# Expert-choice MoE layer on one core: gate and up in chunks of 512 inner columns, and the sample tokens' tiles of two chunks in one block

## The chip, the cores and the metric

The kernel runs on one core of a Trainium2 chip. Its time is the device time in microseconds of one execution; the median of three runs is compared. The profile is of one execution, taken by the hardware profiler.

## The reference

One layer of a bidirectional encoder runs on two request groups with the same weights: a prompt of 1024 tokens and a sample of 256 tokens, model width 1024, all fp32. First comes a mixer (projection to 2048, gated convolution, 2-D Fourier mixing, output projection, two norms). Then comes a mixture of 16 experts with inner width 2816, which takes most of the time. Each expert picks the tokens with the highest affinity to it, 128 of the prompt and 32 of the sample:

```
aff = jax.nn.softmax(logits, axis=-1)
cap = CAPACITY_FACTOR * t // N_EXPERTS          # 128 (prompt), 32 (sample)
gates, idx = lax.top_k(aff.T, cap)
xe = jnp.take(xt, idx, axis=0)
a = jnp.einsum("ecd,edf->ecf", xe, w_gate)      # (16, cap, 1024) x (16, 1024, 2816)
b = jnp.einsum("ecd,edf->ecf", xe, w_up)
ye = jnp.einsum("ecf,efd->ecd", jax.nn.silu(a) * b, w_down)
ye = ye * gates[..., None].astype(ye.dtype)
out = jnp.zeros_like(xt).at[idx.reshape(-1)].add(ye.reshape(-1, d))
```

The layer ends with a final norm of all tokens.

## The kernel before

The first 548 us hold the mixer, the router and the choice of tokens; the change does not touch them. Then the experts follow one after another: expert 0, a hardware loop over experts 1 to 14, and expert 15, all from the same function `expert`, written once per engine.

**Units.** The weights of an expert arrive in 33 units of 1 MB: 22 of the input stage (gate and up) and 11 of the down stage. `load_unit` on SyncE's queue fills a ring `raw` of 11 slots, 8 KB a partition each. An input unit holds 256 inner columns of up and of gate (a chunk, eleven to an expert) for half of the contraction, four of its eight 128-row pieces k; each row of it is a piece of 1 KB in memory. A down unit holds two inner blocks of 128 rows, with pieces of 4 KB. The first four units of expert 0 are loaded early.

**Two products from one load.** For the prompt tokens, each unit is split into a high half `spl_h` (ScalarE, L660) and a low half `spl_l` (VectorE, L1021), three units deep (`SPL`), and TensorE does three matmuls of 512 columns for each product in `three` (L315 to L317): high by high, high by low, low by high. The sample tokens are multiplied in plain fp32 straight from `raw`. They are only 32, so four matmuls share the array: each has 32 stationary columns and goes to its own 32 partitions of bank 2 (`sample_in`, L1289) or, in the down stage, of bank 6 (`sample_down`, L1301).

**Blocks.** TensorE does the sample work in blocks behind certain units. `ENDS` names the ten units that close one: 3, 7, 11, 15, 19 and 21 of the input stage, 24, 27, 30 and 32 of the down stage. In a block of the input stage it first turns the finished products of earlier chunks by transposes (`transposed`, L1263, and `transposed_s`, L1271), then samples the column tile of 512 columns (two chunks of 256) that just ended. Each block ends in one increment of `pe_s`, and only that frees the slots of its units:

```
sp.wait_ge(pe_s, e * BLOCKS + (block_of(i - RAW) + 1))
load_unit(e, i)
```

**Behind TensorE.** At the end of a chunk ScalarE takes silu of the gate half from PSUM (`silu_p`, L672) and only then splits the next unit; VectorE multiplies with the up half (L1031) ahead of its own split. The prompt's up and gate of a chunk share one bank (banks 0 and 1 in turn), the turned products go to banks 7 and 3, the down sums to banks 4 and 5. After unit 24 TensorE turns the gathered tokens of the next expert (`gathered`, L1250). At the expert's end ScalarE scales yP (L704) and yS (L725), and GpSimd adds both to the result in memory by indirect DMA (L494, L498), one after the other. After the last expert the result is read back, normed and written.

## Time and profile before

| | |
|---|---|
| median of three runs | 2610.35 us (2608.66 to 2610.88) |
| profiled execution | 2607.22 us, span 2605.4 us |
| TensorE busy | 2465.3 us (95%) |
| VectorE, ScalarE busy | 1661.5 us (64%), 1360.6 us (52%) |
| chain that ended last | TensorE 91%, VectorE 5%, the rest under 2% each |
| DMA queue of SyncE | 452176 packets, 598.88 MB, 68.0% of 16 engines |
| loads of gate and up | 352 each, 512 KB a load |
| loads of down | 176, 1024 KB a load |
| expert stage | from 548 to 2567 us |

Busy time of TensorE is modelled and its matmuls overlap in it (a mean of 390 ns for a matmul that follows its neighbour by 227 ns), so its cost is read from starts, not from means. A wait is put down to what came last.

### The profile page before, as it was taken

The page shows a single profiled execution, that of the slowest core. Times are in us where ns is not written, and L with a number is a line of the kernel's source. Part 1 is how long each engine was busy: PE and PEld are TensorE (multiplying, and loading weights), DVE is VectorE, ACT ScalarE, POOL GpSimd, SP SyncE. Part 2 cuts the span into 40 slices and gives each one's busy share as a digit, 9 for nine tenths or more (in the row PEclk, how much of TensorE's full clock was granted, in tenths as well). Part 3 has the DMA queues.
Part 4 walks back from the last instruction along what each step waited for, and adds up shares of the span by engine and source line. Part 5 has one row for each costly group of instructions (what it writes and reads, how often), then busy time and mean ns, then how long its engine had stood idle before and what let it go on. Part 6 is the DMA issues. An engine that isn't in the chain of part 4 may idle for free.

```text
span 2605.4 us, 46448 instructions
## 1 busy us (share of the span) xinstructions
PE 2465.3 (95%) x18269; PEld 1903.4 (73%) x18269; DVE 1661.5 (64%) x1541; ACT 1360.6 (52%) x1473; POOL 269.2 (10%) x191
## 2 busy tenths in 40 slices
PE   5999779669999999999999999999999999999994
PEld 4888768547777777777777777777777777777772
DVE  4344456966666666666676666676766676666663
ACT  5222323336555555555565656565555565565553
POOL 0010120010202020202020201111020202020000
PEclk8999989779999999999999999999999999999997
DMA  3110253537979798989798888888888888888885
GB/s 117 41 40 17 106 167 114 178 110 281 294 281 291 277 285 292 284 292 284 279 287 289 280 295 285 286 290 284 270 295 281 292 288 287 292 284 292 256 289 180
DMA packets 460734, 627.31 MB, mean 241 GB/s; under 512 B 21392, under 2 KB 400528, under 8 KB 460304
## 3 DMA queue, kind: packets, MB, share of 16 engines
q1 hardware_dynamic: 452176, 598.88, 68.0%
q0 software_dynamic: 8384, 25.71, 3.9%
q8 instruction: 157, 2.57, 0.4%
q14 instruction: 17, 0.14, 0.0%
HBM read 598.31 MB, written 26.21 MB: 240 GB/s over the span
## 4 chain that ended last, share of the span: by engine, by line
PE 91%; DVE 5%; DMA 1%; ACT 1%; issue 1%; POOL 0%; SPq 0%; POOLq 0%; DVEq 0%; ACTq 0%
PE ps L315 21%; PE ps L316 20%; PE ps L317 20%; PE ps L1289 12%; PE ps L1105 9%; PE ps L1301 6%; PE ps L1263 1%; DVE i L896 1%; DVE v L894 1%; DVE A L898 1%; DMA wo_raw<-in_w_out_dram 1%; PE ps L1250 1%; DVE fo L1083 0%; PE ps L1271 0%; DVE wof_l L834 0%
## 5 line engine op out<-in xcount | busy, mean ns | idle before, releaser
L1021 DVE TENSOR_TENSOR spl_l<-raw,spl_h 128x2048 fp32r<-128x2048 f32 x528 | 1210.1, 2292 | 653.2 <-ACT spl_h L660 633.9
L660 ACT ACTIVATE spl_h<-raw 128x2048 fp32r<-128x2048 f32 x528 | 1010.8, 1915 | 559.5 <-PE ps L317 559.4
L315 PE MATMUL ps<-spl_h,xT 128*128 128x512 f32 x1408 | 559.3, 397 | 2.5 <-DVE xT L1026 2.5
L317 PE MATMUL ps<-spl_h,xT 128*128 128x512 f32 x1408 | 549.8, 390 | 0.0
L316 PE MATMUL ps<-spl_l,xT 128*128 128x512 f32 x1408 | 549.4, 390 | 0.0
L315 PEld LDWEIGHTS ps<-spl_h,xT 128*128 128x128 f32 x1408 | 264.6, 188 | 94.3 <-issue 41.6
L1289 PE MATMUL ps<-raw,xTs 128*32 128x256 f32 (+1 forms) x6144 | 324.1, 363 | 0.0
L317 PEld LDWEIGHTS ps<-spl_h,xT 128*128 128x128 f32 x1408 | 264.7, 188 | 56.0
L316 PEld LDWEIGHTS ps<-spl_l,xT 128*128 128x128 f32 x1408 | 264.8, 188 | 52.4
L315 PE MATMUL ps<-spl_h,g 128*128 128x512 f32 x704 | 281.8, 400 | 0.0
L316 PE MATMUL ps<-spl_l,g 128*128 128x512 f32 x704 | 275.3, 391 | 0.0
L317 PE MATMUL ps<-spl_h,g 128*128 128x512 f32 x704 | 274.2, 390 | 0.0
L1289 PEld LDWEIGHTS ps<-raw,xTs 128*32 128x32 f32 x6144 | 185.2, 110 | 112.3 <-issue 16.1
L494 POOL DMA_INDIRECT acc_dram<-yP,sidx x16 | 26.0, 1624 | 1780.5 <-ACT yP L704 1780.5
L315 PEld LDWEIGHTS ps<-spl_h,g 128*128 128x128 f32 x704 | 132.0, 188 | 49.3 <-issue 22.9
L1301 PE MATMUL ps<-raw,gs 128*32 128x256 f32 x2816 | 165.2, 381 | 0.0
L317 PEld LDWEIGHTS ps<-spl_h,g 128*128 128x128 f32 x704 | 132.2, 188 | 28.6
L316 PEld LDWEIGHTS ps<-spl_l,g 128*128 128x128 f32 x704 | 132.2, 188 | 25.5
L672 ACT ACTIVATE sv<-ps 128x256 f32<-128x256 f32 x176 | 67.7, 385 | 151.5 <-PE ps L317 151.5
L1301 PEld LDWEIGHTS ps<-raw,gs 128*32 128x32 f32 x2816 | 85.0, 110 | 69.1 <-issue 19.6
L1105 PE MATMUL ps<-hT_h,win_h 128*128 128x512 f32 (+1 forms) x384 | 96.4, 359 | 5.9 <-DVE win_l L771 5.9
L1105 PE MATMUL ps<-hT_l,win_h 128*128 128x512 f32 (+1 forms) x384 | 96.2, 359 | 0.0
(195 smaller groups left out, 2170.5 us busy)
## 6 DMA issues: line engine op xcount, KB each, us to landing
raw<-in_w_up_dram SPq DMA_DIRECT2D x352, 512.0 KB, 6.1
raw<-in_w_gate_dram SPq DMA_DIRECT2D x352, 512.0 KB, 7.3
raw<-in_w_down_dram SPq DMA_DIRECT2D x176, 1024.0 KB, 8.8
win_raw<-in_w_in_dram SPq DMA_DIRECT2D x16, 512.0 KB, 3.8
xt<-in_x_dram SPq DMA_DIRECT2D x10, 512.0 KB, 8.2
xr<-in_x_dram SPq DMA_DIRECT2D x10, 512.0 KB, 4.0
acc_dram<-xr SPq DMA_DIRECT2D x10, 512.0 KB, 2.6
xn_dram<-xn SPq DMA_DIRECT2D x10, 512.0 KB, 2.9
```

Source lines behind the costliest of these rows:

```text
L315: eng.matmul(o, a_h, b_h, start=first, stop=False, skip_group_check=True)
L316: eng.matmul(o, a_h, b_l, start=False, stop=False, skip_group_check=True)
L317: return eng.matmul(o, a_l, b_h, start=False, stop=last, skip_group_check=True)
L660: act.activation(spl_h[:, i % SPL, :], raw[:, slot_of(i), :], ACT.Copy).then_inc(sh_ok, 1)
L672: act.activation(sv[:, :], bank(c % 2)[:, FW:2 * FW], ACT.Silu).then_inc(s_ok, 1)
L894: dve.max(v[0:n, rs], A[0:n, :]).then_inc(top_ok[h], 1)
L896: dve.max_index(idx[0:n, rs], v[0:n, rs], A[0:n, :]).then_inc(top_ok[h], 1)
L898: dve.match_replace(A[0:n, :], v[0:n, rs], A[0:n, :], -2.0).then_inc(top_ok[h], 1)
L1021: dve.tensor_tensor(spl_l[:, i % SPL, :], raw[:, slot_of(i), :], spl_h[:, i % SPL, :].bitcast(F32), ALU.subtract).then_inc(sl_ok, 1)
L1105: last = pe.matmul(u[:, t0:t1], w[:, slot, k, :], h[:, k, t0:t1], start=(k == 0 and i == 0), stop=(k == KD - 1 and i == 2), skip_group_che ...
L1289: last = pe.matmul(o, xTs[:, k, :], w, start=k == 0, stop=k == KD - 1, skip_group_check=True)
L1301: last = pe.matmul(bank(6)[q * CAPS:(q + 1) * CAPS, 0:DQ], gs[:, f, :], raw[:, slot_of(i), b * D + q * DQ:b * D + (q + 1) * DQ], start=f = ...
```

## The change

Gate and up come in six chunks: chunk 0 has 256 inner columns in two units as before, chunks 1 to 5 have 512 in four units each, every unit with two k of them. The rows of a wide chunk are pieces of 2 KB. The prompt's up and gate of a wide chunk have a bank each (banks 4 and 5 for odd chunks, 0 and 1 for even ones), and three matmuls of 512 columns go to the one, three to the other for each k. Chunk 0 has bank 3. The down sums move to banks 0 and 1, the gathered tokens' transposes to banks 4 and 5.

The sample work is done in five blocks, behind units 5, 13, 21, 28 and 32. A block of the input stage samples two chunks, into the two halves of bank 2. `pe_s` still rises once for each chunk sampled, and once for each down block, so that a chunk's slots come free when its own sampling is done. silu, product and turned halves are done once a chunk, 512 columns wide. `TURNS` names the block in which each chunk is turned. `sv`, `svs` and `pvs` get new places.

The core of the diff:

```diff
@@ -29,15 +29,21 @@
 E = 16
 F = 2816
 FB = F // P
-NC = FB // 2
+HID = 4 * P
+NC = F // HID + 1
+INS = 4 * NC - 2
 CAP, CAPS = 2 * SEQ // E, 2 * DEC // E
 C = CAP + CAPS
-UNITS = 3 * NC
+UNITS = INS + FB // 2
 FW = 2 * P
 KH = KD // 2
-BATCHES = (NC + 1) // 2
-ENDS = [min(4 * b + 3, 2 * NC - 1) for b in range(BATCHES)] + [2 * NC + 2, 2 * NC + 5, 2 * NC + 8, UNITS - 1]
-BLOCKS = len(ENDS)
+LASTS = [1 + 4 * c for c in range(NC)]
+BATCH = ((0, 1), (2, 3), (4, 5))
+NB = len(BATCH)
+DOWNS = (INS + 6, UNITS - 1)
+ENDS = [LASTS[b[-1]] for b in BATCH] + list(DOWNS)
+TURNS = [min(n for n in range(len(ENDS)) if ENDS[n] > LASTS[c]) for c in range(NC)]
+SAMPLE = NC + len(DOWNS)
 UNIT = 2 * D
 QS = P // CAPS
 DQ = D // QS
...
@@ -165,10 +171,10 @@
         xgs = at("xgs", 90 * KB, [P, DQ])
         yP = at("yP", 94 * KB, [P, D])
         yS = at("yS", 98 * KB, [P, DQ])
-        pv = at("pv", 110 * KB, [P, 3, FW])
-        sv = at("sv", 113 * KB, [P, FW])
-        svs = at("svs", 114 * KB, [P, P])
-        pvs = at("pvs", 114 * KB + 512, [P, P])
+        pv = at("pv", 110 * KB, [P, 3, HID])
+        sv = at("sv", 108 * KB, [P, HID])
+        svs = at("svs", 205 * KB, [P, 2, P])
+        pvs = at("pvs", 75 * KB, [P, 2, P])
 
         fx = at("fx", 117 * KB, [P, TILES, D])
...
+        def first_block(c):
+            return 4 * c - 2 if c else 0
+
+        def blocks(c):
+            return 4 if c else 2
+
+        def first_unit(c):
+            return LASTS[c - 1] + 1 if c else 0
+
+        def chunk_of(i):
+            return (i + 2) // 4
+
+        def up_bank(c):
+            if c == 0:
+                return bank(3)[:, 0:FW]
+            return bank((0, 4)[c % 2])
+
+        def gate_bank(c):
+            if c == 0:
+                return bank(3)[:, FW:2 * FW]
+            return bank((1, 5)[c % 2])
+
+        def turned(c):
+            return bank((3, 7)[c % 2])[:, 0:blocks(c) * P].rearrange("p (b n) -> p b n", b=blocks(c))
+
+        def turned_s(b):
+            return bank(3 if b == NB - 1 else 6)
+
+        def batch_blocks(b):
+            first = first_block(BATCH[b][0])
+            return first, sum(blocks(c) for c in BATCH[b])
+
         def three(eng, o, a_h, a_l, b_h, b_l, first, last):
 
             eng.matmul(o, a_h, b_h, start=first, stop=False, skip_group_check=True)
...
@@ -353,14 +391,17 @@
 
 
             def load_unit(e, i):
-                if i < 2 * NC:
-                    fs = slice((i // 2) * FW, (i // 2 + 1) * FW)
-                    ks = slice((i % 2) * KH, (i % 2 + 1) * KH)
-                    dst = raw[:, slot_of(i), :].rearrange("p (k f) -> p k f", k=KH)
-                    sp.dma_start(dst[:, :, 0:FW], up_v[e, :, ks, fs]).then_inc(raw_in[slot_of(i)], 16)
-                    sp.dma_start(dst[:, :, FW:2 * FW], gate_v[e, :, ks, fs]).then_inc(raw_in[slot_of(i)], 16)
+                if i < INS:
+                    c = chunk_of(i)
+                    w, kn = blocks(c) * P, KD // blocks(c)
+                    fs = slice(first_block(c) * P, first_block(c) * P + w)
+                    r = i - first_unit(c)
+                    ks = slice(r * kn, (r + 1) * kn)
+                    dst = raw[:, slot_of(i), :].rearrange("p (k f) -> p k f", k=kn)
+                    sp.dma_start(dst[:, :, 0:w], up_v[e, :, ks, fs]).then_inc(raw_in[slot_of(i)], 16)
+                    sp.dma_start(dst[:, :, w:2 * w], gate_v[e, :, ks, fs]).then_inc(raw_in[slot_of(i)], 16)
                 else:
-                    j = i - 2 * NC
+                    j = i - INS
...
+            def released(i):
+                if i < INS:
+                    return chunk_of(i) + 1
+                return NC + min(n for n in range(len(DOWNS)) if DOWNS[n] >= i) + 1
 
             for i in range(EARLY, UNITS):
                 if i >= RAW:
-                    sp.wait_ge(pe_s, block_of(i - RAW) + 1)
+                    sp.wait_ge(pe_s, released(i - RAW))
                 load_unit(0, i)
             with nc.Fori(1, E, engines=(sp.engine,), hint_back_edge=True) as e:
                 for i in range(UNITS):
                     if i < RAW:
-                        sp.wait_ge(pe_s, e * BLOCKS + (block_of(i - RAW + UNITS) + 1 - BLOCKS))
+                        sp.wait_ge(pe_s, e * SAMPLE + (released(i - RAW + UNITS) - SAMPLE))
                     else:
-                        sp.wait_ge(pe_s, e * BLOCKS + (block_of(i - RAW) + 1))
+                        sp.wait_ge(pe_s, e * SAMPLE + released(i - RAW))
                     load_unit(e, i)
...
             def silu_p(e, c):
-                act.wait_ge(pe_unit, e * UNITS + (2 * c + 2))
-                if not (isinstance(e, int) and e == 0 and c == 0):
-                    act.wait_ge(p_ok, e * NC + c)
-                act.activation(sv[:, :], bank(c % 2)[:, FW:2 * FW], ACT.Silu).then_inc(s_ok, 1)
+                act.wait_ge(pe_unit, e * UNITS + (LASTS[c] + 1))
+                act.activation(sv[:, 0:blocks(c) * P], gate_bank(c), ACT.Silu).then_inc(s_ok, 1)
 
             def silu_s(e, b):
-                act.wait_ge(pe_s, e * BLOCKS + (b + 1))
-                if not (isinstance(e, int) and e == 0 and b == 0):
-                    act.wait_ge(pS_ok, e * BATCHES + b)
-                if b < BATCHES - 1:
-                    act.activation(svs[:, :], bank(2)[:, P:2 * P], ACT.Silu).then_inc(sS_ok, 1)
+                act.wait_ge(pe_s, e * SAMPLE + (BATCH[b][-1] + 1))
+                n = len(BATCH[b])
+                if b == 0:
+                    act.activation(svs[0:64, 0, :], bank(2)[64:P, 0:P], ACT.Silu).then_inc(sS_ok, 1)
+                    act.activation(svs[:, 1, :], bank(2)[:, FW + P:2 * FW], ACT.Silu).then_inc(sS_ok, 1)
                 else:
-                    act.activation(svs[0:64, :], bank(2)[64:P, 0:P], ACT.Silu).then_inc(sS_ok, 1)
+                    act.activation(svs[:, 0:n, :], bank(2)[:, 0:n * FW].rearrange("p (n m f) -> p n m f", n=n, m=2)[:, :, 1, :],
+                                   ACT.Silu).then_inc(sS_ok, 1)
 
             def product_hi(e, c):
                 act.wait_ge(pT_ok, e * NC + (c + 1))
-                gb = g[:, 2 * c * GB:(2 * c + 2) * GB].rearrange("p (b n) -> p b n", b=2)
-                act.activation(gb[:, :, P:2 * P], bank((7, 3)[c % 2])[:, 0:FW].rearrange("p (b n) -> p b n", b=2),
-                               ACT.Copy).then_inc(gh_ok, 1)
+                f, w = first_block(c), blocks(c)
+                gb = g[:, f * GB:(f + w) * GB].rearrange("p (b n) -> p b n", b=w)
+                act.activation(gb[:, :, P:2 * P], turned(c), ACT.Copy).then_inc(gh_ok, 1)
 
             def product_s(e, b):
-                act.wait_ge(sT_ok, e * BATCHES + (b + 1))
-                if b < BATCHES - 1:
-                    act.wait_ge(pT_ok, e * NC + (2 * b + 2))
-                w = 4 if b < BATCHES - 1 else 2
-                act.activation(gs[:, 4 * b:4 * b + w, :], bank(3)[:, FW:FW + w * CAPS].rearrange("p (b n) -> p b n", b=w),
+                f, w = batch_blocks(b)
+                act.wait_ge(sT_ok, e * NB + (b + 1))
+                act.activation(gs[:, f:f + w, :], turned_s(b)[:, 0:w * CAPS].rearrange("p (b n) -> p b n", b=w),
                                ACT.Copy).then_inc(gs_ok, 1)
...
+                    if i in LASTS:
+                        silu_p(e, LASTS.index(i))
...
+                    if i in ENDS:
                         b = ENDS.index(i)
-                        if b > 0:
+                        for c in range(NC):
+                            if TURNS[c] == b:
+                                product_hi(e, c)
+                        if 0 < b <= NB:
                             product_s(e, b - 1)
-                            product_hi(e, 2 * b - 1)
-                        if b < BATCHES - 1:
-                            product_hi(e, 2 * b)
-                        silu_s(e, b)
-                    if i == ENDS[BATCHES]:
-                        product_s(e, BATCHES - 1)
-                        product_hi(e, NC - 1)
-                        if not last:
+                        if b < NB:
+                            silu_s(e, b)
...
+            dve.memset(pvs[:, 0, :], 0.0).then_inc(pS_ok, 1)
...
+            def prompt_in(e, i):
+                c = chunk_of(i)
+                w, kn = blocks(c) * P, KD // blocks(c)
+                for kk in range(kn):
+                    k = (i - first_unit(c)) * kn + kk
+                    u = slice(kk * 2 * w, (kk + 1) * 2 * w)
+                    wh, wl = spl_h[:, i % SPL, u], spl_l[:, i % SPL, u]
+                    if c == 0:
+                        last = three(pe, bank(3), xT[:, 0, k, :], xT[:, 1, k, :], wh, wl, k == 0, k == KD - 1)
+                    else:
+                        for m, o in enumerate((up_bank(c), gate_bank(c))):
+                            ms = slice(m * w, (m + 1) * w)
+                            last = three(pe, o, xT[:, 0, k, :], xT[:, 1, k, :], wh[:, ms], wl[:, ms], k == 0, k == KD - 1)
+                last.then_inc(pe_unit, 1)
...
+            def sample_in(e, c, n):
+                w, kn = blocks(c) * P, KD // blocks(c)
                 for k in range(KD):
+                    i = first_unit(c) + k // kn
+                    u = raw[:, slot_of(i), (k % kn) * 2 * w:(k % kn + 1) * 2 * w]
                     for q in range(QS):
-                        if b < BATCHES - 1:
-                            unit = 4 * b + 2 * (q // 2) + k // KH
-                            w = raw[:, slot_of(unit), (k % KH) * 2 * FW:(k % KH + 1) * 2 * FW]
-                            w = w.rearrange("p (m h f) -> p h m f", m=2, h=2)[:, q % 2, :, :]
-                            o = bank(2)[q * CAPS:(q + 1) * CAPS, 0:2 * P]
+                        o = bank(2)[q * CAPS:(q + 1) * CAPS, n * FW:(n + 1) * FW]
+                        if c == 0:
+                            o, v_ = o[:, 0:P], u[:, q * P:(q + 1) * P]
                         else:
-                            unit = 4 * b + k // KH
-                            w = raw[:, slot_of(unit), (k % KH) * 2 * FW + q * P:(k % KH) * 2 * FW + (q + 1) * P]
-                            o = bank(2)[q * CAPS:(q + 1) * CAPS, 0:P]
-                        last = pe.matmul(o, xTs[:, k, :], w, start=k == 0, stop=k == KD - 1, skip_group_check=True)
+                            v_ = u.rearrange("p (m f) -> p m f", m=2)[:, :, q * P:(q + 1) * P]
+                        last = pe.matmul(o, xTs[:, k, :], v_, start=k == 0, stop=k == KD - 1, skip_group_check=True)
                 last.then_inc(pe_s, 1)
 
-            def sample_down(e, n):
-                if n == 0:
-                    pe.wait_ge(yS_ok, e + 1)
-                first, end = (2 * NC if n == 0 else ENDS[BATCHES + n - 1] + 1), ENDS[BATCHES + n]
-                pe.wait_ge(gs_ok, e * BATCHES + ((end - 2 * NC) // 2 + 1))
...
+            def turn(e, c):
+                pe.wait_ge(p_ok, e * NC + (c + 1))
+                if c or not (isinstance(e, int) and e == 0):
+                    pe.wait_ge(gl_ok, e * NC + max(c - 1, 0))
+                for b in range(blocks(c)):
+                    last = pe.transpose(turned(c)[:, b, :], pv[:, c % 3, b * P:(b + 1) * P], ident[:, :])
+                last.then_inc(pT_ok, 1)
+
...
+                    if i == 0:
+                        pe.wait_ge(xTl_ok, e + 1)
+                        if later:
+                            pe.wait_ge(gs_ok, e * NB)
+                    if i == first_unit(2) and later:
+                        pe.wait_ge(yP_ok, e)
+                    if i < INS:
+                        prompt_in(e, i)
                     else:
-                        j = i - 2 * NC
-                        pe.wait_ge(gl_ok, e * NC + (j + 1))
-                        if j == 0 and not (isinstance(e, int) and e == 0):
-                            pe.wait_ge(yP_ok, e)
-                        for b in range(2):
-                            f = 2 * j + b
-                            p_lo, p_hi = g[:, f * GB:f * GB + P], g[:, f * GB + P:(f + 1) * GB]
-                            for n in range(2):
-                                ds = slice(b * D + n * 512, b * D + (n + 1) * 512)
-                                last = three(pe, bank(4 + n), p_hi, p_lo, spl_h[:, slot, ds], spl_l[:, slot, ds],
-                                             f == 0, f == FB - 1)
-                    last.then_inc(pe_unit, 1)
-                    if i in ENDS[0:BATCHES]:
-                        b = ENDS.index(i)
-                        if b > 0:
-                            transposed_s(e, b - 1)
-                            transposed(e, 2 * b - 1)
-                        if b < BATCHES - 1:
-                            transposed(e, 2 * b)
-                        sample_in(e, b)
-                    if i in ENDS[BATCHES:]:
-                        if i == ENDS[BATCHES]:
-                            transposed_s(e, BATCHES - 1)
-                            transposed(e, NC - 1)
-                            if not last_expert:
-                                gathered(e + 2)
-                        sample_down(e, ENDS.index(i) - BATCHES)
+                        f = 2 * (i - INS) + 1
+                        pe.wait_ge(gl_ok, e * NC + (min(c for c in range(NC) if first_block(c) + blocks(c) > f) + 1))
+                        prompt_down(e, i)
+                    if i not in ENDS:
+                        continue
+                    b = ENDS.index(i)
+                    for c in range(NC):
+                        if TURNS[c] == b:
+                            turn(e, c)
+                    if b == 1 and later:
+                        pe.wait_ge(yS_ok, e + 1)
+                    if 0 < b <= NB:
+                        turn_s(e, b - 1)
+                    if b == NB and not last_expert:
+                        gathered(e + 2)
+                    if b == 0:
+                        pe.wait_ge(xTs_ok, e + 1)
+                    if b < NB:
+                        for n, c in enumerate(BATCH[b]):
+                            sample_in(e, c, n)
+                    else:
+                        first = INS if b == NB else ENDS[b - 1] + 1
+                        f = 2 * (i - INS) + 1
+                        pe.wait_ge(gs_ok, e * NB + (min(n for n in range(NB) if sum(batch_blocks(n)) > f) + 1))
+                        sample_down(e, first, i)
```

## Rows read from the trace of the kernel before

**Rows 1.** The stretch of one expert; columns in the first line; busy times in us.

```profile
core 0: us, PE busy (x) PEld busy (x) DVE busy (x) ACT busy (x) POOL busy (x), PEclk, DMA share, GB/s
1264.50:1390.68 126.18, 126.18 (x995) 94.99 (x995) 85.25 (x62) 74.55 (x73) 14.21 (x10) 1.00 0.86 285
```

**Rows 2.** The waits of the expert stage, 548 to 2567 us.

```profile
DVE spl_l L1021 <- ACT spl_h L660: 633.9, 443, 4.7
...
PE ps L315 <- DVE xT L1026: 2.5, 1, 2.5
PEld ps L315 <- DVE spl_l L1021: 0.4, 1, 0.4
```

**Rows 3.** Part 5 of the page, three of the costliest groups: busy us, mean ns of one | idle before.

```profile
L1021 DVE TENSOR_TENSOR spl_l<-raw,spl_h 128x2048 fp32r<-128x2048 f32 x528 | 1210.1, 2292 | 653.2 <-ACT spl_h L660 633.9
...
L1289 PE MATMUL ps<-raw,xTs 128*32 128x256 f32 (+1 forms) x6144 | 324.1, 363 | 0.0
...
L1301 PE MATMUL ps<-raw,gs 128*32 128x256 f32 x2816 | 165.2, 381 | 0.0
```

**Rows 4.** The chain of waits of two experts: start us, us, what.

```profile
1207.28 3.59 PE ps L1289 x64
...
1262.61 1.88 PE ps L1289 x64
1264.50 0.43 PE ps L315
1273.21 0.87 PE ps L1250 x8
1274.30 2.73 PE ps L1301 x48
...
1305.01 1.86 PE ps L1301 x32
...
1390.68 0.43 PE ps L315
```

**Rows 5.** The timeline of TensorE around a sample block: start us, us.

```profile
1206.34 0.39 PE L317 MATMUL ps<-spl_h,xT 128*128 128x512 f32 x1
...
1207.21 3.66 PE L1289 MATMUL ps<-raw,xTs 128*32 128x256 f32 x64
...
1211.61 0.39 PE L315 MATMUL ps<-spl_h,xT 128*128 128x512 f32 x1
...
1221.59 0.39 PE L317 MATMUL ps<-spl_h,xT 128*128 128x512 f32 x1
```

**Rows 6.** The same around a block of the down stage.

```profile
1285.03 0.39 PE L317 MATMUL ps<-spl_h,g 128*128 128x512 f32 x1
...
1288.89 0.40 PE L315 MATMUL ps<-spl_h,g 128*128 128x512 f32 x1
```

**Rows 7.** The timeline of SyncE's DMA queue.

```profile
1211.07 0.37 SPq L360 DMA_DIRECT2D raw<-in_w_up_dram  x1
1211.54 0.46 SPq L361 DMA_DIRECT2D raw<-in_w_gate_dram  x1
```

**Rows 8.** The DMA issues of L361, 1211 to 1226 us, issue to landing.

```profile
DMA to landing us min/median/max: 5.0/6.9/8.7
```

**Rows 9.** Two stretches of transfers alone; columns as in rows 1.

```profile
1218.00:1219.00 1.00, 1.00 (x6) 0.84 (x5) 0.55 (x3) 0.85 (x1) 0.00 (x0) 1.00 1.10 346
1248.00:1250.00 2.00, 2.00 (x10) 1.68 (x9) 1.55 (x3) 1.55 (x2) 0.00 (x0) 1.00 1.02 416
```

**Rows 10.** The timeline of ScalarE at the end of a chunk.

```profile
1216.65 0.39 ACT L672 ACTIVATE sv<-ps 128x256 f32<-128x256 f32 x1 [0.88 <-PE ps L317]
1216.93 1.91 ACT L660 ACTIVATE spl_h<-raw 128x2048 fp32r<-128x2048 f32 x1
```

**Rows 11.** The chain of waits at the end.

```profile
2565.84 1.12 ACT yP L704
...
2569.63 6.19 DMA acc_dram<-yS,sidx
```

More of the change, by code:

```diff
@@ L703, in expert @@
                         act.wait_ge(cg_ok, e * 4 + 4)
-                        act.activation(yP[:, :], bank(4, 2), ACT.Copy, scale=cgate[:, 0:1]).then_inc(yP_ok, 1)
+                        act.activation(yP[:, :], bank(0, 2), ACT.Copy, scale=cgate[:, 0:1]).then_inc(yP_ok, 1)
                     n = i + SPL
@@ L1044, in expert @@
+                gb = g[:, f * GB:(f + w) * GB].rearrange("p (b n) -> p b n", b=w)
+                dve.tensor_tensor(gb[:, :, 0:P], turned(c), gb.bitcast(F32)[:, :, P:2 * P], ALU.subtract).then_inc(gl_ok, 1)
             def expert(e, last):
                 for i in range(UNITS):
-                    if i < 2 * NC and i % 2:
-                        product(e, i // 2)
+                    if i in LASTS:
+                        product(e, LASTS.index(i))
                     n = i + SPL
@@ L1253, in gathered @@
                 last.then_inc(xg_ps, 1)
-            def transposed(e, c):
-                pe.wait_ge(p_ok, e * NC + (c + 1))
-                if c >= 2:
-                    pe.wait_ge(gl_ok, e * NC + (c - 1))
-                elif c == 0 and not (isinstance(e, int) and e == 0):
-                    pe.wait_ge(gl_ok, e * NC)
-                for b in range(2):
-                    bs = slice(b * P, (b + 1) * P)
-                    last = pe.transpose(bank((7, 3)[c % 2])[:, bs], pv[:, c % 3, bs], ident[:, :])
-                last.then_inc(pT_ok, 1)
@@ new lines, in prompt_down @@
+            def prompt_down(e, i):
+                for b in range(2):
+                    f = 2 * (i - INS) + b
+                    p_lo, p_hi = g[:, f * GB:f * GB + P], g[:, f * GB + P:(f + 1) * GB]
+                    for n in range(2):
+                        ds = slice(b * D + n * 512, b * D + (n + 1) * 512)
+                        last = three(pe, bank(n), p_hi, p_lo, spl_h[:, i % SPL, ds], spl_l[:, i % SPL, ds],
+                                     f == 0, f == FB - 1)
+                last.then_inc(pe_unit, 1)
@@ L1304, in sample_down, with turn_s @@
                 last.then_inc(pe_s, 1)
+            def turn(e, c):
[5 more added lines that the diff above has]
+                last.then_inc(pT_ok, 1)
+            def turn_s(e, b):
+                pe.wait_ge(pS_ok, e * (NB + 1) + (b + 3))
+                if b or not (isinstance(e, int) and e == 0):
+                    pe.wait_ge(gs_ok, e * NB + b)
+                o = 0
+                for n, c in enumerate(BATCH[b]):
+                    last = pe.transpose(turned_s(b)[:, o:o + P], pvs[:, n, :], ident[:, :])
+                    o += blocks(c) * CAPS
+                last.then_inc(sT_ok, 1)
@@ L1306, in expert @@
             def expert(e, last_expert):
+                later = not (isinstance(e, int) and e == 0)
                 for i in range(UNITS):
                     pe.wait_ge(sl_ok, e * UNITS + (i + 1))
[L1309 to L1332 removed]
```

81 lines of the change are left out of this document (30 added, 51 removed).

## The prediction

> **What bounds the kernel now.** I read the split by engine over one expert first. From one expert's first down matmul to the next's is 126.18 us, TensorE is busy for all of it at granted clock 1.00 (its upper level, 2.4 GHz), VectorE for 85.25 us, ScalarE for 74.55 us, and the DMA engines' mean share is 0.86 [rows 1]. Sixteen such stretches are 2019 of the 2605.4 us. Then the waits: between 548 and 2567 us TensorE waits once for data, 2.5 us at the very start, and its weight loads 0.4 us, while VectorE waits 633.9 us for ScalarE [rows 2]. The reader is to see that nothing feeds TensorE late, so the time is the sum of what TensorE issues. Last, the chain of waits and TensorE's timeline, to find in that sum what is not arithmetic.
>
> The prices, start to start. A 128x512 matmul: 44 of them from 1211.61 to 1221.59, 0.2268 us [rows 5]. A transpose: 8 in 0.87, 0.109 us. A 256-wide sample instruction: 48 take 2.73 and 32 take 1.86, so 0.0544 each and 0.12 us fixed; 64 take 3.59, which gives 0.11 fixed. The 128-wide ones: (1.88 - 0.11) / 64 = 0.0277 [rows 4]. (Each fp32 sample matmul of the source is two instructions.)
>
> Now a whole switch to sample work and back. From the last prompt matmul (1206.34) to the fourth after the block (1211.61) is 5.27 us; it holds four matmuls (0.907), five transposes (0.545) and 64 sample instructions (3.482), together 4.93, so **0.34 us belong to the switch** [rows 5, 4]. In the down stage, with no transposes, 1285.03 to 1288.89 is 3.86 us against 0.907 + 48 x 0.0544 = 3.52: again 0.34 [rows 6]. As a check, an expert has 396 prompt matmuls (22 units and 11 units of 12), 38 transposes, 5 x 64 and 176 wide and 64 narrow sample instructions: 89.8 + 4.1 + 17.4 + 9.6 + 1.8 = 122.7 us. What is left of 126.18 is 3.5 us, over ten blocks 0.35 each.
>
> **The change, part by part.**
>
> *Blocks, ten to five.* ENDS had six blocks in the input stage and four in the down stage; it now has units 5, 13, 21, 28 and 32. The matmuls, transposes and sample instructions of an expert stay the same in number and width (a chunk of 512 has two matmuls of 512 in place of one per k, over half as many k per unit). Five switches an expert go: 5 x 16 x 0.34 = 27.2 us. With 0.35, from the check, it is 28.0.
>
> The row shows that the 0.34 us come alike with transposes and without, and whether 48 or 64 instructions follow; so I take them as a price of the change of kind, paid once a block however long. The Trainium skill (TensorEngine Tiling (Array Packing), Key Properties) says that "Changing tiling mode (not just tile) drains the TensorE". By that the two chunks sampled one after the other, both in 32-column tiles, cost nothing between them, and the sum stays 27.2 us; if instead each chunk's sampling paid its fixed part, it would be the second rival below.
>
> *The last expert's tail.* The chain ends through yP, GpSimd's queue and the DMA of yS, which starts 3.8 us after yP [rows 11]. The sample work behind the last prompt matmul is hidden there: 32 instructions before, 64 after. So 32 x 0.0544 = 1.74 us more lie behind yP, and only about 0.3 us of it show (the block then ends 0.2 + 3.5 us behind the last prompt matmul, yS takes some 0.4 like the equally wide sv [rows 10], together 4.2 with the signal, against 0.2 + 3.8 = 4.0 us at which the queue comes free). Gain 1.4 us.
>
> *Wider silu, product and halves.* Eleven pairs of evictions become six, wider; VectorE and ScalarE lose about 2 us of work per expert each, and gain nothing for the end, since they have 41 and 52 us free [rows 1]. Without that cover it would still be a gain. What counts is their lead at a chunk's end that no block follows (units 9 and 17). The silu starts 0.27 us into the next unit (1216.65 against 1211.61 + 21 x 0.2268 = 1216.37), the split 0.28 us behind it [rows 10]. At 512 columns the silu is longer by about 256 x (1.12 - 0.39) / 768 = 0.24 us, with the 1024-wide yP as the far row [rows 10, 11]. So the split starts at 0.79, takes 1.91, VectorE's half 2.29 [rows 3], and it is ready at 5.0 us; TensorE wants it after two units, at 5.44. Covered, by 0.4 us. Priced at nothing; with the cover gone, what it is late by, 32 times.
>
> *Two accumulators in turn.* In a wide chunk TensorE alternates between two banks every three matmuls. The down stage does so now, and its matmuls run at the same 0.2268 us at clock 1.00. The Trainium skill (TensorE: Matmul & The Clock Gate, A second HAM failure mode) says that cycling through banks can make the clock swing between its levels; here the trace disagrees, and only a small chance stays for it.
>
> *Pieces of 2 KB and the ring of 11 slots.* This is the edit that could cost. SyncE waits for a slot until its sampling is done, and a block now holds 6 to 8 units in place of 4. Take block 1 (units 6 to 13), T being the end of its prompt work. Units 14 to 16 are there; unit 17 waits for chunk 2's sampling. That ends at 0.1 (today's gap ahead of the first sample instruction, 1207.21 - 1206.34 - 0.227 - 0.545) + 10 x 0.109 + 0.12 + 3.48 = T + 4.8 [rows 5, 4]. Today the first gate piece goes out at 1211.54 and lands 5.0 us later, 1216.5, which is 5.7 us after the sampling ended at 1210.87 [rows 4, 7, 8]: unit 17 lands at T + 10.5. The others follow at the rate of the transfers: 346 GB/s with 1 KB pieces, or 3.0 us for the 1.05 MB of a unit, and 416 GB/s with the 4 KB pieces of the down weights, 2.5 us [rows 9]. 2 KB has no row; it lies between, and I take the middle, 2.75 us. TensorE ends chunk 3's sampling at T + 8.3 and unit 14 at 11.1; ScalarE can take unit 17 at 11.4, and each next one 2.72 us later, with 0.9 us to spare (1.92 + 2.29 against two units, 5.44, and the 0.27 of the signal). The last of the batch, 21, may land as late as 11.4 + 10.9 + 0.9 = T + 23.2. It lands at 10.5 + 4 x 2.75 = 21.5; at today's rate 22.5. Covered either way; the ring starts to hurt above 3.17 us a unit. The same walk after unit 21 brings 4 KB pieces, which are faster; after unit 28 seven slots free at once ahead of 22 us of work. The waits that are added (gs_ok, gl_ok, yP_ok, yS_ok) are for work finished a block earlier.
>
> *Sum.* 27.2 + 1.4 = **28.6 us** off the profiled execution's 2607.22 us (span 2605.4, 1.8 us around it): 2578.6. That execution lies 3.1 us under the median shown, so on the median's scale 2610.35 - 28.6 = 2581.7; I say 2581.5.
>
> **Rivals.**
> 1. *The ring starves TensorE (the other side).* For: 11 slots, 8 held, only 3 ahead, and the DMA's mean share is 0.86 already. Against: the walk above. Place: units 17 to 21. Its price is 16 x 4 x (r - 3.17) us with r the time of a unit. It eats all the gain at r = 3.62 us, 290 GB/s. At r = 3.8, slower than any steady stretch of rows 9, it is 40 us: 2621.7. A mild form, r = 3.3, gives 8 us: 2590.
> 2. *The fixed 0.12 us stay with each chunk's sampling.* Then the three merges of the input stage bring 0.22 each: 48 x 0.12 = 5.8 us less gain, 2587.5. Against: rows 5 and 6 price a switch alike.
> 3. *The lead at chunk ends is gone.* For: 0.4 us is little, and VectorE's wider product stands ahead of its split. 0.3 us late, 32 times: 9.6 us, 2591.
> 4. *The clock falls with the banks in turn.* If wholly, the 240 wide-chunk matmuls of an expert would take twice 0.2268 us: +871 us, about 3450.
> 5. *The change moves nothing*: some wait I have not found takes 1.5 to 2 us an expert back, 2605 to 2615.
>
> **How the numbers follow.** Forecast 0.70 (its own range 2579 to 2585: a switch from 0.32 to 0.36 us, and 1.5 us of scatter), rival 2 0.07, rival 3 0.06, rival 1 mild 0.05 and strong 0.06, rival 4 0.01, rival 5 0.05. The range is to hold the first four, 0.88 of the chance, up to 13 us above the forecast: 2576 to 2595. The lower end is a switch of 0.35 and a profile-like execution. 0.2% (5.2 us) is about what a measurement of this kernel tells from no change. Faster: 0.70 + 0.07 + 0.06 + 0.05 = 0.88; same: rival 5, 0.05; slower: strong rival 1 and rival 4, 0.07.
>
> **What would show it.** Right: an expert takes 124.5 us; five blocks in the chain of waits, with 128 sample instructions at 0.0544 (or 0.0277) us behind each other and no gap where the second chunk begins; a first L315-like matmul of 0.43 us five times an expert, not ten. TensorE still waits for nothing. Wrong: waits of TensorE for VectorE's lower half at units 17 to 21 (rival 1, with SyncE's issues bunched after each block) or at units 12 and 20 (rival 3); a second 0.1 us inside the blocks (rival 2). The transfers between two blocks should run above 346 GB/s; if they run below 330 the walk of the ring fails.

## The result and the profile after

The changed kernel takes **2579.67 us** (median of 4 runs, 2579.22 to 2580.67) against 2609.81 us for the kernel before (4 runs, 2608.66 to 2610.88): 30.1 us less, ratio 0.9885, 95% interval 0.9868 to 0.9902. The forecast was 2581.5 us, range 2576 to 2595. The profiled execution took 2579.22 us with a span of 2577.3 us, 28.1 us under the span before.

One expert in the split by engine, the row that answers to [rows 1]:

```profile
core 0: us, PE busy (x) PEld busy (x) DVE busy (x) ACT busy (x) POOL busy (x), PEclk, DMA share, GB/s
1158.92:1283.44 124.52, 124.52 (x996) 95.61 (x995) 84.49 (x50) 73.57 (x56) 8.11 (x10) 1.00 0.80 290
```

TensorE is still busy for the whole of it at granted clock 1.00, VectorE and ScalarE have 0.8 and 1.0 us less to do, and the DMA engines' share fell from 0.86 to 0.80 though they move the same bytes. The chain of waits over that expert (start us, us, what), beside [rows 4]:

```profile
1152.74 6.18 PE ps L1344 x112
1158.92 0.43 PE ps L353
...
1170.05 3.59 PE ps L1344 x64
...
1190.54 5.34 PE ps L1336 x128
...
1219.00 7.04 PE ps L1336 x128
1226.04 0.43 PE ps L353
...
1249.16 7.04 PE ps L1336 x128
...
1277.26 6.18 PE ps L1344 x112
1283.44 0.43 PE ps L353
```

Five blocks in place of ten. The sample instructions keep their price: 64 more in a wide block cost 7.04 - 3.59 = 3.45 us, 0.0539 each, and 112 take 6.18 where 112 x 0.0544 is 6.09. Over many experts, by the transposes of the gathered tokens, which come once an expert (14 of them from the first to the last row, from the same view over 700 to 2500 us):

```profile
778.39 0.87 PE ps L1295 x8
...
2396.02 0.87 PE ps L1295 x8
```

(2396.02 - 778.39) / 13 = 124.43 us an expert against 126.18 [rows 1]: 1.75 us less, 0.35 for each of the five switches that went. Sixteen times that is 28.0 us. The intervals are not all alike. Five of these thirteen are 124.44 to 124.64 us, the others 124.38 or 124.39, for instance

```profile
1649.33 0.87 PE ps L1295 x8
...
1773.72 0.87 PE ps L1295 x8
```

and the one before the first row is 125.37. Together the fourteen are 1.7 us longer than fourteen of the shortest. So an expert that is not held up takes 124.38 us, 1.80 less than before, and the runs below show what that is made of.

A switch by itself in TensorE's timeline, beside [rows 5]:

```profile
1217.51 0.39 PE L355 MATMUL ps<-spl_h,xT 128*128 128x512 f32 x1
1217.74 1.03 PE L1354 MATMUL ps<-ident,pv 128*128 128x128 f32 x8
1218.61 0.38 PE L1363 MATMUL ps<-ident,pvs 128*128 128x128 f32 x2
1218.92 7.11 PE L1336 MATMUL ps<-raw,xTs 128*32 128x256 f32 x128
...
1226.79 0.40 PE L353 MATMUL ps<-spl_h,xT 128*128 128x512 f32 x1
```

From 1217.51 to 1226.79 is 9.28 us; four matmuls (0.91), ten transposes (1.09) and 128 sample instructions (6.96) are 8.96. The switch costs 0.32 us by this count (0.34 in the rows before), although the block is twice as long and samples two chunks.

What changed for the worse is in the waits from 545 to 2545 us:

```profile
ACT spl_h L704 <- DMA raw<-in_w_gate_dram: 122.0, 122, 3.1
...
PE ps L353 <- DVE xT L1065: 2.5, 1, 2.5
...
PE ps L353 <- DVE spl_l L1060: 0.7, 1, 0.7
```

ScalarE now waits for the transfers 122 times, which it did not do before. TensorE feels it once by itself, for 0.7 us, and its weight loads wait four times, 2.0 us in all (0.4 before, [rows 2]); the uneven intervals above say that 1.7 us of the experts' time were lost. How near it is shows in ScalarE's timeline (the splits of units 17, 18 and 21, then of unit 5 of the next expert; the brackets hold the idle time before and its releaser):

```profile
1229.06 1.92 ACT L704 ACTIVATE spl_h<-raw 128x2048 fp32r<-128x2048 f32 x1 [2.57 <-PE ps L355]
1232.19 1.92 ACT L704 ACTIVATE spl_h<-raw 128x2048 fp32r<-128x2048 f32 x1 [1.21 <-DMA raw<-in_w_gate_dram]
...
1240.32 1.92 ACT L704 ACTIVATE spl_h<-raw 128x2048 fp32r<-128x2048 f32 x1 [0.69 <-DMA raw<-in_w_gate_dram]
...
1307.35 1.92 ACT L704 ACTIVATE spl_h<-raw 128x2048 fp32r<-128x2048 f32 x1 [1.30 <-DMA raw<-in_w_gate_dram]
```

With T = 1217.74, the end of the block's prompt work, unit 17 is taken at T + 11.3, unit 18 at 14.5 and unit 21 at 22.6, the last two as soon as they land. The forecast's walk had 11.4 for the first, and let unit 18 land at 10.5 + 2.75 = 13.3 and unit 21 at 21.5, with 23.2 as the limit: both came 1.1 to 1.2 us later than it said, and 0.6 us of cover is left in place of 1.7. Unit 5 is ready at 1307.35 + 1.92 + 0.03 + 2.29 = 1311.6, and TensorE starts it at 1311.82: 0.2 us of cover, at a place that the walk had called ample.

The transfers, a stretch of 2 KB pieces alone (columns as above), beside [rows 9]:

```profile
1206.00:1208.00 2.00, 2.00 (x11) 1.65 (x10) 1.71 (x1) 1.20 (x3) 0.00 (x0) 1.00 1.05 384
```

384 GB/s, between the 346 of 1 KB pieces and the 416 of 4 KB, and a unit takes 2.73 us. The page counts 296891 packets in place of 460734.

The end, beside [rows 11], from the timeline:

```profile
2537.77 1.11 ACT L745 ACTIVATE yP<-ps,cgate 128x1024 f32<-128x1024 f32 x1 [6.18 <-PE ps L355]
...
2541.39 0.47 ACT L764 ACTIVATE yS<-ps,cgate 128x256 f32<-128x256 f32 x1 [2.51 <-PE ps L1344]
2542.66 1.55 POOL L542 DMA_INDIRECT acc_dram<-yS,sidx  x1 [1.40 <-ACT yS L764]
```

The add of yS starts 4.9 us behind yP, not 3.8. Before, yS was ready when GpSimd came free from the add of yP; now GpSimd waits 1.4 us for yS.

### The profile page after: what moved, and what is told of

It reads as the page before. It is cut to its first block, busy times and chain, and to the rows that moved or that the text cites. A ratio compares the mean times of both kernels' runs of the same rounds, so it can differ in the third digit from the quotient of the medians.

```text
span 2577.3 us, 45156 instructions
## 1 busy us (share of the span) xinstructions
PE 2438.6 (95%) x18269; PEld 1915.0 (74%) x18269; DVE 1650.2 (64%) x1350; ACT 1344.1 (52%) x1233; POOL 194.7 (8%) x191
## 2 busy tenths in 40 slices
DMA packets 296891, 627.28 MB, mean 243 GB/s; under 512 B 21392, under 2 KB 72848, under 8 KB 296464
## 4 chain that ended last, share of the span: by engine, by line
PE 90%; DVE 5%; DMA 2%; ACT 1%; issue 1%; SPq 0%; POOL 0%; DVEq 0%; ACTq 0%; POOLq 0%
PE ps L353 20%; PE ps L354 19%; PE ps L355 19%; PE ps L1336 12%; PE ps L1150 9%; PE ps L1344 6%; PE ps L1354 1%; DVE i L935 1%; DVE v L933 1%; DVE A L937 1%; DMA raw<-in_w_gate_dram 1%; PE ps L1295 1%; DMA wo_raw<-in_w_out_dram 1%; DVE wof_l L873 0%; PE ps L1363 0%
## 5 line engine op out<-in xcount | busy, mean ns | idle before, releaser
L1336 PE MATMUL ps<-raw,xTs 128*32 128x256 f32 (+1 forms) x6144 | 314.2, 362 | 0.0
L1344 PE MATMUL ps<-raw,gs 128*32 128x256 f32 x2816 | 158.6, 380 | 0.0
L1150 PE MATMUL ps<-hT_h,win_l 128*128 128x512 f32 (+1 forms) x384 | 96.2, 359 | 0.0
```

Of the source, the lines that this page charges most:

```text
L1150: last = pe.matmul(u[:, t0:t1], w[:, slot, k, :], h[:, k, t0:t1], start=(k == 0 and i == 0), stop=(k == KD - 1 and i == 2), skip_group_che ...
L1336: last = pe.matmul(o, xTs[:, k, :], v_, start=k == 0, stop=k == KD - 1, skip_group_check=True)
L1344: last = pe.matmul(bank(6)[q * CAPS:(q + 1) * CAPS, 0:DQ], gs[:, f, :], raw[:, slot_of(i), b * D + q * DQ:b * D + (q + 1) * DQ], start=f = ...
```

## The experiments

Two theories stood against each other: the gain is the price of the switches between prompt and sample work, or it is the wide chunks (2 KB pieces, six wide evictions in place of eleven pairs). Each run below is timed against the kernel before on the same chip; its own median stands with the ratio's interval. The runs were made in batches on different chips; the kernel before had medians of 2609.4 to 2609.9 us in them, so a difference from the changed kernel's 2579.67 carries about 0.5 us from there, and a median also holds what changes outside the expert stage.

**Four down blocks in the changed kernel.**

```diff
-DOWNS = (INS + 6, UNITS - 1)
+DOWNS = (INS + 2, INS + 5, INS + 8, UNITS - 1)
```

> The changed kernel, but the down stage has four sample blocks again (behind units 24, 27, 30 and 32) in place of two; all else stays, the wide chunks too. Theory (a switch of TensorE between prompt and sample work costs 0.34 us, and the change gains by having fewer of them): 2 x 16 x 0.34 = 10.9 us, and 1.4 us because less sample work hides behind yP at the end: 2579.7 + 12.3 = 2592. Rival (the gain comes from the wide chunks: 2 KB pieces, fewer and wider evictions): within 2 us of 2579.7.

Measured: 2593.32 us, ratio 0.9937 (0.9924 to 0.9951), 13.7 us over the changed kernel. This is the theory of the switches; the rival of the wide chunks (within 2 us of 2579.7) fails. Its experts are all of one length, by the same rows:

```profile
1271.06 0.87 PE ps L1295 x8
...
1396.24 0.87 PE ps L1295 x8
```

125.18 us, 0.80 above the 124.38 of the changed kernel: 0.40 for each of the two down blocks.

**Two down blocks in the kernel before.**

```diff
-ENDS = [...] + [2 * NC + 2, 2 * NC + 5, 2 * NC + 8, UNITS - 1]
+ENDS = [...] + [2 * NC + 6, UNITS - 1]
```

> The kernel before, with one thing of the change alone: the down stage has two sample blocks (behind units 28 and 32) in place of four; chunks stay at 256 columns and 1 KB pieces. Theory of the switch: 2609.8 - 10.9 - 1.4 = 2597.5. Rival of the wide chunks: 2609.8, no change.

Measured: 2595.65 us, ratio 0.9946 (0.9933 to 0.9960), 14.2 us under the kernel before. One line of the old kernel, changed, brings nearly half of the gain, with 256-wide chunks and 1 KB pieces. Its experts all take 125.39 or 125.40 us, 0.79 less than 126.18: again 0.40 a down block.

**Six input blocks in the changed kernel.** Behind a chunk's last unit that closes no block:

```diff
+if i in LASTS and i not in ENDS:
+    b = LASTS.index(i) // 2
+    if b == 0:
+        pe.wait_ge(xTs_ok, e + 1)
+    else:
+        pe.wait_ge(pS_ok, e * (NB + 1) + (b + 2))
+    sample_in(e, BATCH[b][0], 0)
...
-for n, c in enumerate(BATCH[b]):
-    sample_in(e, c, n)
+sample_in(e, BATCH[b][1], 1)
```

> The changed kernel, but each chunk is sampled right behind its own last unit: six sample blocks in the input stage in place of three; the transposes stay where they are. Theory of the switch: 3 x 16 x 0.34 = 16.3 us more, 2596. If the fixed 0.12 us of a block belong to each chunk's sampling (my second rival), they are paid already and only 0.22 us a block come back: 10.6 us, 2590. Rival of the wide chunks: 2579.7. The transfers should also start earlier, so ScalarE should wait less for them.

Measured: 2598.38 us, ratio 0.9956 (0.9942 to 0.9969), 18.7 us over the changed kernel, 0.39 for each of 48 blocks. My second rival (0.22 a block, 2590) is out. Its shortest intervals are 125.46 us, 1.08 above the changed kernel's: 0.36 for each of three input blocks. ScalarE's waits for gate transfers fell from 122.0 us to 52.2 us in the profile's waits.

**Ten blocks, wide chunks.** Both edits together.

> The changed kernel with both of the above: ten sample blocks an expert as before the change, but wide chunks. It closes the account. Theory of the switch: 2579.7 + 16.3 + 12.3 = 2608.3, so the wide chunks by themselves are worth 1.5 us or less against 2609.8. Rival of the wide chunks: near 2580, nearly all the gain stays.

Measured: 2611.90 us, ratio 1.0007 (0.9998 to 1.0016). That is 3.6 us over the theory's 2608.3 and about 2 us over the kernel before: with ten blocks the wide chunks gain nothing. The two edits add up (13.7 + 18.7 = 32.4 us, and both together cost 32.2). All its experts take 126.26 us:

```profile
1276.16 0.87 PE ps L1295 x8
...
1402.42 0.87 PE ps L1295 x8
```

So the wide chunks cost 0.08 us an expert, the two down switches are worth 126.26 - 125.46 = 0.80 and the three input switches 126.26 - 125.18 = 1.08, and 0.80 + 1.08 - 0.08 = 1.80 us is what the change takes off an expert that is not held up.

**What a switch is made of: the transposes between the two samplings.**

```diff
+if b < NB:
+    sample_in(e, BATCH[b][0], 0)
 for c in range(NC):
     if TURNS[c] == b:
         turn(e, c)
...
 if b < NB:
-    for n, c in enumerate(BATCH[b]):
-        sample_in(e, c, n)
+    sample_in(e, BATCH[b][1], 1)
```

(with a wait for xTs_ok or pS_ok ahead of the first sampling)

> The changed kernel, but in the three input blocks the transposes (full array, fp32) stand between the sampling of the block's first and second chunk, in place of ahead of both. The same instructions, and the slots of the first chunk come free up to 1.1 us earlier. It asks what the 0.34 us belong to. Theory (to the change between full-width work and 32-column tiles): one more change there and back in each input block, 48 x 0.34 = 16.3 us, 2596. Rival (to the change between the split prompt data and plain fp32, which the transposes share with the sample work): no change, 2580.

Measured: 2593.11 us, ratio 0.9939 (0.9925 to 0.9952), 13.4 us over the changed kernel or 0.28 for each of the 48 spells (by its shortest intervals, 125.10 and 125.11, it is 0.24). TensorE's timeline of this kernel:

```profile
1221.55 3.66 PE L1336 MATMUL ps<-raw,xTs 128*32 128x256 f32 x64
1225.14 1.09 PE L1354 MATMUL ps<-ident,pv 128*128 128x128 f32 x8
1226.07 0.38 PE L1363 MATMUL ps<-ident,pvs 128*128 128x128 f32 x2
1226.38 3.66 PE L1336 MATMUL ps<-raw,xTs 128*32 128x256 f32 x64
```

Each 64 now take 3.59 us (0.11 over 64 x 0.0544), and the ten transposes 1.24 instead of 1.09. So most of the price is paid when full-width work and 32-column tiles change places, also where both are plain fp32. The kind of the data doesn't explain it alone. Whether the 0.1 us between these 0.24 to 0.28 and the 0.36 of an input switch belongs to the split data was not tried, nor what in the change costs: a tile's place in the array, or the narrower weight loads.

**How near the ring is: 1 KB pieces.** Each load of a wide chunk in two DMAs, by columns; and as a control in two DMAs by k.

```diff
+for h in range(2 if c else 1):
+    n = 2 * P
+    o = first_block(c) * P + h * n
+    sp.dma_start(dst[:, :, m * w + h * n:m * w + (h + 1) * n],
+                 src[e, :, ks, o:o + n]).then_inc(raw_in[slot_of(i)], 16)
```

> The changed kernel, but every load of a wide chunk is cut by columns into two DMAs of 1 KB pieces (four DMAs a unit; same bytes, same places, same blocks). It asks how much cover the ring has. In the trace of the changed kernel ScalarE takes unit 18 at 14.5 us and unit 21 at 22.6 us behind the block's last prompt matmul, both times released by the DMA, where my walk had 13.3 and 21.5; the limit was 23.2. At the 346 GB/s of 1 KB pieces (3.0 us a unit in place of 2.7) unit 21 comes 1.5 us later, at 24.1: TensorE waits 0.9 us an expert, 14 us, 2594. My walk on record, 22.5 at this rate, says covered: 2580.

> The control of the 1 KB run: also four DMAs a unit, but cut by k, so that the pieces stay at 2 KB. If the size of the pieces is what counts: within 2 us of 2579.7. If it is the number of DMAs that SyncE issues, it is as slow as the 1 KB run.

Measured: with 1 KB pieces 2616.85 us, ratio 1.0024 (1.0014 to 1.0035); the control 2582.91 us, ratio 0.9895 (0.9880 to 0.9910). The control is 3.2 us over the changed kernel, more than the 2 I allowed, but its trace does not put this on the four DMAs a unit: from the first prompt matmul of the experts to the last yP it takes 1988.79 us (549.89 to 2538.68), the changed kernel 1989.01 (548.76 to 2537.77). The difference lies in the mixer and behind the experts. Against the control the pieces' size costs 34 us, more than the whole gain, and far more than either of my numbers. The chain of waits of the 1 KB kernel shows where:

```profile
1163.86 6.22 PE ps L1349 x112
...
1202.71 5.34 PE ps L1341 x128
...
1231.17 3.63 PE ps L1341 x64
...
1262.25 7.04 PE ps L1341 x128
1290.35 6.23 PE ps L1349 x112
...
1332.25 5.34 PE ps L1341 x128
```

From the block of unit 28 to that of the next expert's unit 5 it takes 38.85 and 41.90 us; the changed kernel has 1190.54 - 1152.74 = 37.80. From the block of unit 13 to that of 21 it takes 31.08 against 30.16. The second is what I had worked out, 0.9 us. The first I had not looked at: the freed slots are filled there without a pause, while GpSimd's gather and adds use the same engines. In this kernel's split by engine:

```profile
1189.00:1192.00 3.00, 3.00 (x15) 2.49 (x14) 2.31 (x2) 2.20 (x3) 2.13 (x1) 1.00 1.03 238
1216.00:1219.00 3.00, 3.00 (x15) 2.49 (x14) 2.58 (x2) 1.92 (x1) 0.00 (x0) 1.00 1.10 348
...
1327.00:1332.00 5.00, 4.59 (x14) 3.48 (x14) 3.39 (x3) 3.18 (x3) 0.00 (x0) 0.66 1.10 348
```

With GpSimd's DMA at work (2.13 us busy in the first) the engines are as full but move 238 GB/s, not 348. The changed kernel shows the same with 2 KB pieces: 261 GB/s from 1303 to 1306 us, with GpSimd busy for 2.69 us, against 384. How much of the loss is the sharing and how much the slower pieces was not separated.

The third row holds something else. TensorE had just waited 2.35 us, until 1327.41; behind that the mean granted clock is 0.66, a stretch at the lower level, 1.2 GHz, in which seven matmuls follow each other by 0.43 us in place of 0.23, 1.4 us lost. So this wait cost more than its own length, and the two are most of the 4.1 us that this expert lost there (41.90 - 37.80). The trace has one more such stretch, in the second expert; the changed kernel has none between 560 us and the end of the experts.

**The down slots free earlier.** Blocks behind 27 and 32 in place of 28 and 32, once in the changed kernel and once with 1 KB pieces.

```diff
-DOWNS = (INS + 6, UNITS - 1)
+DOWNS = (INS + 5, UNITS - 1)
```

> The changed kernel, but the down blocks stand behind units 27 and 32 in place of 28 and 32: still five blocks, six and five down units in them, so that the first down slots come free 3.5 us earlier (one unit of 2.72 us and 16 sample instructions less). TensorE's work is the same. In the changed kernel ScalarE takes unit 5 of the next expert when the DMA lets it, and its two halves are ready at about 1311.6 us, where TensorE wants it at 1311.8: hardly covered, yet covered. Theory: 2579.7, at most 1 us less. Rival (small waits there still cost the changed kernel something that its trace hides): 2575 to 2578.

> The 1 KB run (2616.9 us) with the down blocks behind 27 and 32. In the 1 KB run's chain of waits an expert loses about 1.3 us between its predecessor's block of unit 28 and its own first block, where the transfers run without a pause and the gather and the adds of GpSimd go over the same engines, and about 0.75 us between the blocks of units 13 and 21. Theory (both places are ring starvation, and the first goes when its slots come free 3.5 us earlier): 16 x 1.3 = 21 us less, 2596. Rival (1 KB pieces are too slow by their mean rate, so that the loss only moves to the next block): within 5 us of 2616.9.

Measured: 2579.93 us, ratio 0.9887 (0.9872 to 0.9902), for the first: the same as the changed kernel by the median. Its trace says a little more: its experts all take 124.40 or 124.41 us, so the 1.7 us that the changed kernel's profiled execution lost in places are not lost here. The medians are too coarse to tell whether the thin cover costs that. 2590.41 us, ratio 0.9931 (0.9917 to 0.9944), for the second: 26.4 us less than with the block behind 28. So most of the 34 us was starvation at the expert's start. What is left, 10.5 us over the same blocks with 2 KB pieces or 0.66 an expert, is of the size of the other place. The kernel before with two down blocks has 1 KB pieces too, and its even experts show no loss; there a sample block behind unit 3 stands ahead of unit 5, so that unit 5 is wanted later.

**Slots given back by the block.**

```diff
-return chunk_of(i) + 1
+return chunk_of(i) // 2 * 2 + 2
```

> The changed kernel, but the slots of a block's units are given back only when both of its chunks are sampled, in place of chunk by chunk; TensorE's work is the same. The transfers of units 17 and on then start 3.5 us later. Theory (the ring has well under 2 us to spare behind a wide block, and the finer release is what keeps TensorE fed): unit 21 comes at 26.1 against a limit of 23.2, so TensorE waits 2.9 us there, and about as long behind the block of unit 21: 16 x 5.8 = 93 us, 2672; if the 4 KB pieces of the down stage make up for the second, 2626. Rival (the ring has cover to spare, the release doesn't matter): 2580.

Measured: 2654.52 us, ratio 1.0171 (1.0157 to 1.0185): 74.9 us over the changed kernel, 4.7 an expert. The chain of waits:

```profile
1241.15 7.09 PE ps L1336 x128
...
1272.92 7.09 PE ps L1336 x128
...
1302.51 6.18 PE ps L1344 x112
```

Here 31.77 us from unit 13's block to unit 21's (30.16 in the changed kernel) and 29.59 from there to unit 28's (28.10). TensorE waits at both places, as forecast, but about half as long each here. Other experts lose more: in the next one the second stretch takes 33.39 us,

```profile
1400.60 7.09 PE ps L1336 x128
...
1433.99 6.18 PE ps L1344 x112
```

with a granted clock of 0.66 from 1420 to 1425 us, behind the wait. The release chunk by chunk is a necessary part of the change.

**Silu three times as long.**

```diff
-act.activation(sv[:, 0:blocks(c) * P], gate_bank(c), ACT.Silu).then_inc(s_ok, 1)
+w = blocks(c) * P
+act.activation(sv[:, :, 0:w], gate_bank(c).unsqueeze(1).broadcast_to([P, 3, w]), ACT.Silu).then_inc(s_ok, 1)
```

> The changed kernel, but silu goes over its columns three times in one instruction (1536 in place of 512; the product uses the last third), so ScalarE is about 1.0 us longer at each chunk's end. The changed kernel's trace has the split of unit 20 ready 0.44 us before TensorE wants it. Theory (that lead is 0.4 us at units 12 and 20 and ample elsewhere): 1.0 - 0.44 = 0.55 us late, 32 times, 17.5 us, 2597. Rival (ScalarE's work at a chunk's end is hidden anyway, as its 52% of busy time suggests): 2580.

Measured: 2598.08 us, ratio 0.9953 (0.9940 to 0.9967), 18.4 us over the changed kernel, 0.575 for each of 32. In its waits:

```profile
PE ps L353 <- DVE spl_l L1061: 7.5, 32, 0.2
```

32 waits of TensorE, two an expert. They are 0.23 us each; the weight loads' own waits (23.8 us in 42) stand beside them. From the first prompt matmul to the last yP this kernel takes 2005.98 us, 0.53 more for each of the 32. An engine that is busy 52% of the time has 0.44 us to spare at these two places.

## Why the prediction was right

**TensorE's sum bounds it.** Right: it stays busy throughout, at clock 1.00, and the stage shrank by what it no longer issues. The two accumulators in turn left the clock alone (mean granted clock 1.00 from 548 to 2536 us). What the Trainium skill (TensorE: Matmul & The Clock Gate, A second HAM failure mode) reports of another kernel that cycled through banks did not show here.

**0.34 us a switch, 80 of them, 27.2 us.** Right, and slightly low. By the interval from expert to expert an input switch is 0.36 us and a down switch 0.40:

| kernel | expert to expert, us |
|---|---|
| before, ten blocks | 126.18 to 126.19 |
| wide chunks, ten blocks | 126.26 |
| wide chunks, six input and two down blocks | 125.46 to 125.73 |
| before, two down blocks | 125.39 to 125.40 |
| wide chunks, three input and four down blocks | 125.18 |
| changed kernel | 124.38 to 124.64, one 125.37 |

The term should have been 16 x 1.88 = 30.1 us in place of 27.2. Two things that the forecast had at nothing stand against it: 16 x 0.08 = 1.2 us for the wide chunks and the 1.7 us of waits. 30.1 - 1.2 - 1.7 is 27.2 again, and that the three cancel is luck. From the first prompt matmul of the experts to the last yP the profiled executions took 2017.88 and 1989.01 us, 28.9 less; 16 x 1.80 + 1.74 (sample work moved behind yP) - 1.7 is 28.8.

Part of a switch's price hangs on the block's length after all: the fixed part that I took for constant is 0.11 us for 64 sample instructions and 7.04 - 128 x 0.0544 = 0.08 for 128. On the number of chunks in a block it does not hang: nothing shows where the second begins. The Trainium skill's sentence (TensorEngine Tiling (Array Packing), Key Properties) that changing the tiling mode drains TensorE, and changing the tile does not, agrees with the run of the transposes in between: 0.24 to 0.28 us for a spell of full-width work inside a block, and nothing visible where the second chunk follows the first. That it is a draining that takes this time, no run here shows.

**1.4 us at the tail.** Right in kind, too large. Of the 1.74 us moved behind yP, 1.1 showed in place of 0.3 (4.9 - 3.8 us): between the end of yS and the start of its add lie 2542.66 - 2541.86 = 0.8 us for signal and issue, which I had set near nothing. The term is about 0.6 us. The medians can't show it: behind the add of yS the profiled executions themselves differ by 1.1 us (35.8 and 34.6 to the end).

**Silu, product and halves at nothing.** Right, though the work that VectorE and ScalarE lose is 0.8 and 1.0 us an expert, not 2. The lead at a chunk's end, worked out as 0.4 us from the width of yP, was 0.44, and the run that used it up lost what it should.

**The ring.** For the changed kernel right in the main: 1.7 us are lost over the fourteen intervals, with one wait of 0.7 us. The rate for 2 KB pieces, guessed at 2.75 us a unit, is 2.73. But three things in the step were wrong. The units behind the first landed 1.1 us later than the walk said. "Covered either way", said of today's 1 KB rate, fails: with these five blocks that rate costs 34 us, and even at the place walked 22.5 + 1.1 is past the limit of 23.2. And the stretch behind unit 28, put aside as seven slots at once ahead of 22 us of work, is the tightest place of all, 0.2 us at unit 5. I had walked one block from a full ring and had left out that the transfers there share the engines with the gather and the adds. That the time came out right owes something to the 2 KB pieces: they bring no gain of their own, and with 1 KB pieces the same five blocks would have given nothing (2616.85 us).

**What stays open.** Why a switch costs 0.40 us in the down stage and 0.36 in the input stage was not settled, nor what the 0.08 us of the wide chunks are. Nor was it tried whether another order of the down blocks could give the ring room enough for fewer than five: with 11 slots and three units split ahead a block can hold eight, and 33 units in four blocks don't fit.

## What to carry to other kernels

On an engine that never waits, look for what its instructions don't account for: multiply counts by start-to-start spacings, and ask what the remainder is counted in. Here it was counted in changes between full-width matmuls and column tiles, and batching the small ones halved it. Then ask what the longer batch holds back: walk the ring through every stage of a cycle, the one with foreign DMA traffic first, and free what can be freed before the batch ends.

## What the runs showed of the hardware

A change from full-width matmuls to 32-column tiles and back cost TensorE 0.32 to 0.40 us, and transposes of full width set between two spells of tiles cost 0.24 to 0.28 us extra, though both were plain fp32. Loads by SyncE's queue moved 348 GB/s with 1 KB pieces, 384 with 2 KB and 416 with 4 KB; with GpSimd's indirect DMA on the same engines, 3 us passed at 238 GB/s with the engines' share still at 1.03. Behind a wait of TensorE of 2.35 us the granted clock was 0.66 over 5 us, and matmuls followed each other by 0.43 us in place of 0.23.
